# Fourteen modulation units inside three norms, paired units at the first norm, and the step sizes' columns beside the rotated keys

## What is computed

```python
for i in range(DEPTH):                                  # 2 layers
    mod = s_lat @ w_mod[i] + b_mod[i]                   # 1024 -> 6 * 1024
    mod_c = s_ctx @ w_mod[i] + b_mod[i]
    x, xc = _layer(x, xc, mod, mod_c, rope, i < DEPTH - 1, p)

def _layer(x, xc, mod, mod_c, rope, need_ctx, p):
    sh1, sc1, g1, sh2, sc2, g2 = jnp.split(mod[:, None, :], N_MOD, axis=-1)
    h = _modulate(_rms_norm(x, p['g_pre_mix']), sh1, sc1)        # h * (1 + scale) + shift
    hc = _modulate(_rms_norm(xc, p['g_pre_mix']), csh1, csc1)
    ua, us, um = _split_in(h @ p['w_in'])   # ua: queries, keys/values; um ends with the step sizes dt
    ...                                     # latent attention, short convolution, state-space scan
    y = jnp.concatenate([y_att, y_sc, y_ssd], axis=-1) @ p['w_out']
    x = x + g1 * _rms_norm(y, p['g_post_mix'])
    h = _modulate(_rms_norm(x, p['g_pre_ffn']), sh2, sc2)
    f = jnp.square(jax.nn.relu(h @ p['w_ff1'])) @ p['w_ff2']
    x = x + g2 * _rms_norm(f, p['g_post_ffn'])
```

## Time and profile before

| what | us |
|---|---|
| median of 3 runs | 1782.94 |
| lowest and highest of them | 1777.03 and 1785.53 |
| the profiled execution | 1776.61 |
| its span in the trace | 1774.8 |
| its mean granted clock of PE, share of full speed | 0.927 |

### The profile page before, as it was taken

One profiled execution on the slowest core, in us unless ns is written; L12 is line 12 of the kernel. 1 busy time (PEld: TensorE's weight loads), 2 busy tenths in 40 slices (PEclk: granted clock), 3 DMA queues, 4 the chain that ended last, 5 costly groups with the idle time before them and its releaser, 6 DMA issues.

```text
span 1774.8 us, 25783 instructions
## 1 busy us (share of the span) xinstructions
PE 1586.2 (89%) x10259; PEld 1326.2 (75%) x10259; DVE 992.8 (56%) x1598; ACT 917.6 (52%) x1516; POOL 63.7 (4%) x82
## 2 busy tenths in 40 slices
PE   6799988878999999959989789998999999797697
PEld 3578555646888888837955679997989899786587
DVE  0454557555344444454746676667765766576655
ACT  4553555346232323454555555456776766376646
POOL 3000014000000000000004000000000000000000
PEclk8799997788999999969998789998999999989798
DMA  8423364412323223303355436663644434242232
GB/s 276 146 71 95 119 204 153 142 48 71 119 95 95 95 95 96 108 18 96 119 167 190 143 98 195 198 200 129 218 136 143 143 126 134 97 144 95 72 119 72
DMA packets 221560, 225.40 MB, mean 127 GB/s; under 512 B 6154, under 2 KB 219984, under 8 KB 221392
## 3 DMA queue, kind: packets, MB, share of 16 engines
q1 hardware_dynamic: 220736, 223.63, 39.1%
q0 software_dynamic: 704, 0.12, 0.0%
HBM read 222.68 MB, written 1.05 MB: 126 GB/s over the span
## 4 chain that ended last, share of the span: by engine, by line
PE 75%; ACT 11%; DVE 10%; issue 2%; DMA 1%; SPq 0%; DVEq 0%; ACTq 0%; POOL 0%; POOLq 0%
PE bank L851 20%; PE bank L852 20%; PE bank L853 20%; ACT whi L1330 2%; PE bank L1136 2%; PE bank L876 2%; DVE wlo L1869 2%; PE bank L865 1%; ACT SH L1474 1%; PE bank L1114 1%; PE bank L1192 1%; ACT AP L1731 1%; PE bank L1029 1%; PE bank L1021 1%; DVE AP L2378 1%
## 5 line engine op out<-in xcount | busy, mean ns | idle before, releaser
L1869 DVE TENSOR_TENSOR wlo<-raw,whi 128x1024 fp32r<-128x1024 f32 (+3 forms) x322 | 389.0, 1208 | 349.4 <-ACT whi L1330 345.1
L1330 ACT ACTIVATE whi<-raw 128x1024 fp32r<-128x1024 f32 (+3 forms) x322 | 337.2, 1047 | 325.6 <-PE bank L853 305.8
L851 PE MATMUL bank<-HH,whi 128*128 128x512 f32 (+3 forms) x656 | 254.1, 387 | 29.0 <-DVE HL L1891 27.3
L852 PE MATMUL bank<-HL,whi 128*128 128x512 f32 (+3 forms) x656 | 250.9, 382 | 0.0
L853 PE MATMUL bank<-HH,wlo 128*128 128x512 f32 (+3 forms) x656 | 250.5, 382 | 0.0
L851 PE MATMUL bank<-HA,whi 128*128 128x256 f32 x576 | 167.0, 290 | 18.8 <-DVE wlo L1869 8.7
L851 PEld LDWEIGHTS bank<-HH,whi 128*128 128x128 f32 (+2 forms) x656 | 123.6, 188 | 61.6 <-issue 22.3
L852 PE MATMUL bank<-LA,whi 128*128 128x256 f32 x576 | 164.0, 285 | 0.0
L853 PE MATMUL bank<-HA,wlo 128*128 128x256 f32 x576 | 163.9, 284 | 0.0
L853 PEld LDWEIGHTS bank<-HH,wlo 128*128 128x128 f32 (+2 forms) x656 | 123.7, 189 | 26.9 <-issue 1.5
L852 PEld LDWEIGHTS bank<-HL,whi 128*128 128x128 f32 (+2 forms) x656 | 123.9, 189 | 26.1 <-issue 1.8
(11 more groups left out here) (365 smaller groups left out, 3217.1 us busy)
## 6 DMA issues: line engine op xcount, KB each, us to landing
raw<-in_w_ff_dram SPq DMA_DIRECT2D x64, 1024.0 KB, 5.2
raw<-in_w_mod_dram SPq DMA_DIRECT2D x48, 1024.0 KB, 5.2
raw<-in_a_w_in_dram SPq DMA_DIRECT2D x40, 1024.0 KB, 5.0
raw<-in_w_in_dram SPq DMA_DIRECT2D x16, 1024.0 KB, 5.2
raw<-in_b_w_in_dram SPq DMA_DIRECT2D x9, 1024.0 KB, 5.3
raw<-in_w_out_dram SPq DMA_DIRECT2D x8, 1024.0 KB, 5.1
raw<-in_ple_w_gate_dram SPq DMA_DIRECT2D x8, 1024.0 KB, 5.1
raw<-in_a_w_out_dram SPq DMA_DIRECT2D x4, 1024.0 KB, 5.0
```

Of the source, the lines that this page charges most:

```text
L851: nc.tensor.matmul(o, wh, xh, start=start, stop=False, skip_group_check=shared)
L852: nc.tensor.matmul(o, wh, xl, start=False, stop=False, skip_group_check=shared)
L1330: f(whi[h % HALF_SLOTS][:, 0:n], raw[u.id % RAW_SLOTS][:, (h % 2) * n:(h % 2) * n + n], ACT.Copy)\
L1869: v.tensor_tensor(wlo[h % HALF_SLOTS][:, 0:n], raw[u.id % RAW_SLOTS][:, (h % 2) * n:(h % 2) * n + n], whi[h % HALF_SLOTS][:, 0:n].bitcast( ...
```

## The change

It has five parts.

1. The 16 columns of dt are loaded beside the 160 of "kv" by a second transfer into the same slot (runs of 16 values, 64 bytes); the block of 32 becomes one of 48, and "bc" loses its third block. dtT is copied from rows 32 to 47 of the kv block's bank.
2. Fourteen modulation units leave the attention, the scan and w_ff2, and stand inside three norms: 5 in the norm between w_out and w_ff1 of layer 0, 5 in the one between the layers, 4 in the one before w_ff1 of layer 1. They use banks 3 to 6. Two stand before `post`'s sum, one after it, the rest between `norm_sum` and `norm`; ACT and DVE do their rows' work after `post` (two), before `norm_sum` (one) and after `norm` (the rest). The first two weight units after the norm are created and split before `post`. So 19 units stay in layer 0's attention and scan (7 and 12), none in w_ff2, none in layer 1's attention, 7 in layer 1's scan.
3. At the first norm the units come in pairs (shift and scale of the same features), between parts of the sum of squares; kv is split before the last three arrive, the norm is cut in two halves of four feature blocks, and the first half of kv (by feature block) and of q stand between them, with unit 7.
4. `post` no longer adds the last two squares into ACC: PE sums ACC and the two squares. The last two gates are multiplied after the root.
5. The raw slots shrink from 272 to 256 columns a unit.

```diff
 FILL = {
-    "mla": ((1, (1, 8)), (1, (1, 24))),
-    "g": ((1, (1, 8)), (1, (1, 24))),
-    "head": ((1, (1, 8)), (1, (1, 24))),
-    "out": ((1, (1, 8)), (1, (1, 24))),
+    "mla": ((1, (1, 8)), (0, (1, 24))),
+    "g": ((1, (1, 8)), (1, (1, 20))),
+    "head": ((1, (1, 8)), (1, (1, 20))),
+    "out": ((1, (1, 8)), (1, (1, 20))),
 }
+MLA_FILLED = 7
...
+    def kv_unit(l):
+        fm(A["w_in"][l], 0, COL_KV, 160, [(0, P), (P, 48)], "win", (l, "kv"), ("h", l, "mix"), [ALL] * 2, None, [(COL_DT, 16)])
...
-        fm(w, 0, COL_XBC + 512, 272, two + [(256, 16)], "win", (l, "bc"), x, [ALL] * 3)
+        fm(w, 0, COL_XBC + 512, 256, two, "win", (l, "bc"), x, [ALL] * 2)
...
+    one_mod(0)
+    one_mod(4)
+    steps.append(("sum_part", 0, 3))
+    one_mod(1)
+    steps.append(("sum_part", 3, 6))
+    one_mod(5)
+    steps.append(("sum_part", 6, KC))
+    u_kv = without_step(kv_unit, 0)
+    steps.append(("split_to", u_kv))
+    one_mod(2)
+    one_mod(6)
+    one_mod(3)
+    steps.append(("mod_flush",))
+    for j in range(3):
+        steps.append(("fuse_pair", j))
+    steps.append(("norm", 0, "mix", (0, 4)))
+    steps.append(("first_half", u_kv))
+    one_mod(7)
+    u_q = without_step(q_unit, 0)
+    steps.append(("split_to", u_q))
+    steps.append(("first_block", u_q, 0))
+    steps.append(("mod_flush",))
+    steps.append(("fuse_pair", 3))
+    steps.append(("first_block", u_q, 1))
+    steps.append(("norm", 0, "mix", (4, KC)))
...
+        first = [without_step(ff1_unit, 0, i) for i in (0, 1)]
+        made = gap_mods(5 if l == 0 else 4)
+        for u in made[:2]:
+            steps.append(("mod_mm", u))
+        steps.append(("split_to", first[1]))
         steps.append(("post", l, "mix"))
+        for u in made[:2]:
+            steps.append(("mod_rest", u))
+        for u in made[2:3]:
+            steps.append(("unit", u))
         steps.append(("mod_fuse", l, "ffn"))
         steps.append(("norm_sum", l, "ffn"))
-        steps.append(("norm", l, "ffn"))
+        for u in made[3:]:
+            steps.append(("mod_mm", u))
+        steps.append(("norm", l, "ffn", (0, KC)))
+        for u in made[3:]:
+            steps.append(("mod_rest", u))
...
         def post(l, which):
             t = t_of(l)
-            total(s_norm_sum, ("p", l, which), ACC[:, t[0]:t[1]], t[1] - t[0], s_acc, ("p", l, which, KC - 1), (s_inv, ("p", l, which)))
+            b = acquire(7, (s_inv, ("p", l, which)))
+            pe.wait_ge(s_acc, s_acc.at(("p", l, which, KC - 3)))
+            nc.tensor.matmul(b[:, 0:t[1] - t[0]], ones, ACC[:, t[0]:t[1]], start=True, stop=False)
+            for m in (KC - 2, KC - 1):
+                pe.wait_ge(s_sq, s_sq.at(("p", l, which, m)))
+                ins = nc.tensor.matmul(b[:, 0:t[1] - t[0]], ones, SQ[m % 2][:, t[0]:t[1]], start=False, stop=m == KC - 1)
```

More of the change, by code:

```diff
@@ L48 @@
 RAW_SLOTS, HALF_SLOTS = 3, 4
[L49 removed]
+UNIT_COLS = 256
 AHEAD = 4
@@ L457, in build, with fm @@
     units, steps = [], []
-    def fm(w, rows, col, n, blocks, kind, key, x, t, between=None):
-        src = w[rows:rows + D, col:col + n].rearrange("(k p) n -> p k n", p=P)
-        u = Unit(kind, [(0, 8 * n, src)], n, key, len(units), blocks, x, t)
+    def fm(w, rows, col, n, blocks, kind, key, x, t, between=None, more=()):
+        cols = [(col, n), *more]
+        n = sum(m for _, m in cols)
+        loads, at_ = [], 0
+        for c, m in cols:
+            loads.append((0, 8 * n, at_, m, w[rows:rows + D, c:c + m].rearrange("(k p) n -> p k n", p=P)))
+            at_ += m
+        u = Unit(kind, loads, n, key, len(units), blocks, x, t)
         units.append(u)
@@ L496, in build, with q_unit, without_step @@
     two = [(0, P), (P, P)]
+    def kv_unit(l):
+        fm(A["w_in"][l], 0, COL_KV, 160, [(0, P), (P, 48)], "win", (l, "kv"), ("h", l, "mix"), [ALL] * 2, None, [(COL_DT, 16)])
+    def q_unit(l):
+        fm(A["w_in"][l], 0, 0, 256, two, "win", (l, "q"), ("h", l, "mix"), [ALL if l == 0 else X] * 2)
+    def without_step(make, *args):
+        n = len(steps)
+        make(*args)
+        del steps[n:]
+        return units[-1]
     def w_in_units(l):
@@ L581, in build @@
         steps.append(("mod_flush",))
-        steps.append(("post", l, "ffn"))
+        if l == 0:
+            gap_units = [without_step(kv_unit, 1), without_step(q_unit, 1)]
+            made = gap_mods(5)
+            for u in made[:2]:
+                steps.append(("mod_mm", u))
+            steps.append(("split_to", gap_units[1]))
+        else:
+            gap_units, made = [], []
+        steps.append(("post", l, "ffn"))
+        for u in made[:2]:
+            steps.append(("mod_rest", u))
+        for u in made[2:3]:
+            steps.append(("unit", u))
+        for u in first + gap_units if l == 0 else first:
+            u.apart = True
     seq2 = [(0, SEQ)] * 2
@@ L663, in build @@
     mla_last = {l: (l, MLA_HEADS - 1, 1) for l in range(LAYERS)}
-    mod_step = {st[1].key: n for n, st in enumerate(steps) if st[0] == "unit" and st[1].kind == "mod"}
+    mod_step = {st[1].key: n for n, st in enumerate(steps) if st[0] in ("unit", "mod_rest") and st[1].kind == "mod"}
     def half_size(u):
@@ L795, in _ @@
                     sp.wait_ge(s_lo_ready, s_lo_ready.at(2 * before.sid + 1))
-            for off, width, src in u.loads:
+            for off, width, c, m, src in u.loads:
                 dst = raw[u.id % RAW_SLOTS][:, off:off + width].rearrange("p (k n) -> p k n", n=u.n)
-                load(dst, src, raw_in[u.id % RAW_SLOTS])
+                with nc.allow_non_contiguous_dma(reason="sixteen columns of step sizes"):
+                    load(dst[:, :, c:c + m], src, raw_in[u.id % RAW_SLOTS])
             if u.kind == "win" and u.key == (1, "kv"):
@@ L899, in unit @@
                 pe.wait_ge(s_lo_ready, s_lo_ready.at(2 * u.sid + half))
-                for bi, (c0, m) in enumerate(u.blocks):
+                turns = [(bi, kk) for bi in range(len(u.blocks)) for kk in range(4)]
+                if u.by_k:
+                    turns.sort(key=lambda at_: at_[1])
+                for bi, kk in turns:
+                    c0, m = u.blocks[bi]
+                    if only is not None and bi != only:
+                        continue
                     t = u.t[bi]
                     token_major = u.kind == "av" or (u.kind == "bkv" and bi == 1)
-                    if half == 0:
+                    if half == 0 and kk == 0:
                         if u.packed and bi == 0:
@@ L1129, in ssd_out, with norm_sum @@
             ssd_total(l, 1, acquire(4, (s_inv, ("ssd", l, 1))))
-        def norm_sum(l, which):
+        def norm_sum(l, which, k0=0, k1=KC):
             t = ALL if which == "mix" else t_of(l)
-            b = acquire(7, (s_inv, ("n", l, which)))
-            for k in range(KC):
+            b = acquire(7, (s_inv, ("n", l, which))) if k0 == 0 else banks[7]
+            for k in range(k0, k1):
                 pe.wait_ge(s_sq, s_sq.at(("n", l, which, k)))
@@ L1266, in _ @@
                 norm_sum(*args)
+            elif kind == "sum_part":
+                norm_sum(0, "mix", *args)
             elif kind == "rows":
@@ L1410, in unit @@
                         f(ZS[:, 2 * int(part[1]) + bi, t[0]:t[1]], ps, ACT.Silu).then_inc(*key(u.key + (bi,)))
-                    elif part == "bc" and bi == 2:
-                        f(dtT[0:16, :], ps, ACT.Copy).then_inc(*key(u.key + (bi,)))
                     else:
@@ L2542, in _ @@
             if kind == "norm":
-                l, which = args
-                t = ALL if which == "mix" else t_of(l)
-                if which == "mix":
+                l, which, some = args
+                if which == "mix" and some[0] == 0:
                     if l > 0:
```

184 lines of the change are left out of this document (129 added, 55 removed).

## The result

The changed kernel takes **1786.39 us** (median of 20; 1782.77 to 1788.49), the kernel before 1779.95 (20 runs in turn with it): a ratio of 1.0030, 95% interval 1.0017 to 1.0043. It is slower by 0.3%, a small difference but a measured one. I had forecast 1758. In the profiled executions the spans are 1784.9 against 1774.8 us, 10.1 apart.

What follows compares the result with a forecast made beforehand. PE was taken as the bound, three quarters of the chain. Terms -11.1 - 17.7 + 3.6 - 2 + 3.0 - 0.8 = -25.0 gave 1751.6 from the profiled 1776.6, 1758 against the median 1782.94; forecast 1751 to 1764, range 1744 to 1773.

Steps and rivals of the forecast that it cites:

- part 3: Units' cost inside three norms: +3.6 us in sum; those behind norm_sum cost 0, as PE waited 6.75 there.
- rival D: Three norms and the first: mod_rows on ACT behind late loads hold up the norms; slower, about 1785; chance 0.04.
- Parts 2 and 3: Fourteen units leave attention, w_ff2 and layer 1's scan, -17.7 us; their cost inside the norms, +3.6.
- -2 for the clock: Three norms: units in the waits may keep the granted clock up; -2 us, out of 0 to -6.8.
- The third unit: In the three norms: its load lands 5.2 us after issue and squares queue behind it; +0.3, 0 and +3.3 us.
- point (d): Granted clock at the first products after each norm: 0.5 by the forecast, 1.0 by rival B.
- rival B: Norms stay warm: the clock holds at 2.4 GHz there, the first norm too; 1748 us; chance 0.16.
- Part 1: w_in's dt block: four stretches of 2.77 us go, second transfer hidden; -11.1 us (-9 to -11.1).
- Part 5: First norm: first product earlier, -1.9 us, rest up to q's end longer, +4.9; net +3.0 (-1 to +5.5).
- (e): First norm: first product at about 53, q ends at 88, some 4 us wait for HL before kv's second half.
- Part 6: Last post: saves an add and the gates ahead of the root; -0.8 us (0 to -1).
- parts 2, 3 and 4: Units out of dense stretches, -17.7 us; units inside the norms, +3.6; the clock in three norms, -2.

Runs made afterwards that it cites:

- e1: The changed kernel with the second and third units' column products inside the three norms sent to banks 4 and 5, not the rotating banks; 1768.6 us, ratio 0.9939.
- e4: As e1, but no modulation units inside the norms, all fourteen back in the dense stretches; 1770.7 us, ratio 0.9962.
- e3: As e1, but with the first norm of the kernel before; 1765.5 us, ratio 0.9919.
- e9: The kernel before plus the step sizes' columns and the changed post norm, no units in norms, old first norm; 1768.9 us, ratio 0.9928.
- e5: As e3, with the first two units of each of the three norms behind the post norm's sum, on PE only; 1765.2 us, ratio 0.9923.
- e6: As e5, with two units moved from layer 1's norm to the first two steps of layer 1's attention; 1761.9 us, ratio 0.9909.
- e7: As e3, plus 20 unread f32 products, ten ahead of the scores in each of the first two steps of layer 1's attention; 1774.4 us, ratio 0.9978.
- e11: As e8, with the last columns' flush and the gate's fusing moved behind w_out's first unit in both layers; 1757.8 us, ratio 0.9851.
- e8: As e5, with four units per norm, none between post norm and norm's sum, and two in layer 1's attention; 1752.5 us, ratio 0.9852.
- e2: The kernel before with only the step sizes' columns beside the keys and the smaller slots; 1770.9 us, ratio 0.9955.

## Why the prediction was wrong

**The step that failed: part 3, "and PE waited 6.75 there: 0".** I priced the units behind norm_sum by their length on PE against PE's idle time, and asked whether their loads were there. I did not ask where their columns go and when they leave. Each flush takes one of the three banks that the weight products rotate through, and only DVE's copy frees it, which stands behind the norm in DVE's order. The order of the instructions, which I had, shows three flushes ahead of ff1's first product and their copies behind the last HL. The forecast gave this nothing; e1 measures it at 16 us. My rival D had rows on ACT that hold up the norms; it was a queue, a wait and the right sign, but the wrong engine, and the loads were not as late as it needed: the first square came 1.5 us late in layer 0 and 4.5 in layer 1, about as priced with 5.2 us a load. That its 1785 lies next to the measured 1786 is luck: its sum takes the loss of 6.8 us four times, where its text names three norms, and with three it gives 1778.

**Parts 2 and 3, the fourteen units.** I had -17.7 outside, +3.6 inside and -2 for the clock, together -16.1. By the ratios, e1 against e4 gives -4 and e3 against e9 -2. By stages of e3 against e9:
- w_ff2 -1.3 (forecast -1.5): right. Layer 0's attention -5.8 (-5.6) and layer 1's scan -2.2 (-2.4) look right, but by luck. Against e9's 182.6 the same attention is 2.6 to 3.7 us shorter in e5, e6, e7 and e11, and with the new first norm 2.7 (e4 186.4, e1 183.7). The scan with two units less is 1.7 longer than in the kernel before (65.1 against 63.4).
- Layer 1's attention **-4.7, forecast -8.2**. I treated the heads' waits only as time freed or not. Seven units less let PE idle at their head, and the granted clock, 1.00 with a unit in each step, fell to 0.52 over ten us in e3. e6 shows that the first two units there cost 0.2 us together.
- Inside the norms **+12.8, forecast +3.6**: 4.3, 3.1 and 5.5. The third unit was named as the one that decides, and its wait read right (4.60 us on PE; in layer 1 ACT's first square is at 1031.25, 35.7 us behind w_out's first product where it was 31.2, 4.5 late against 4 forecast). Its price was not: e8, without it and with two units back in the attention, has +0.9, +1.1 and -0.3. In layer 0 I took the first square as 1.3 us late and that as made up by XT's last blocks at the end. Nothing was made up: the sixteen records of the sum of squares take 9.6 to 9.7 us on PE with the third unit as without it, and from w_out's first product to the first one behind the norm it is 75.1 us in e3 and 72.0 in e9 and e8. The other 1.1 us at each of the two norms ahead of w_ff1 are a term that I left out. The last two units' flushes stand in the middle of w_ff1, where PE has no wait (timeline of PE, e3):

```profile
425.13 0.95 PE L958 MATMUL bank<-pick,mod_row 128*128 128x2 f32 x8
```

- The clock: at the first product after layer 0's norm it is at the low level, 0.77 us at 400.09 in e1 as at 403.75 before, and with the banks mended the products stay slow for 11.2 us, as before. There point (d) came out as forecast, rival B did not, and the -2 was not there either. Layer 1's norm is different, and (d) fails there: the first product takes 0.36 us, nearer to the 0.28 of the full clock, and the next group starts with 0.58, in the kernel before and in the changed one alike, so nothing was gained (timelines of PE, before and after):

```profile
1032.60 0.36 PE L851 MATMUL bank<-HX,whi 128*128 128x256 f32 x1 [4.13 <-DVE HXL L1891]
...
1042.42 0.36 PE L962 MATMUL bank<-HX,whi 128*128 128x256 f32 x1 [2.59 <-DVE HXL L2037]
1044.04 0.58 PE L962 MATMUL bank<-HX,whi 128*128 128x256 f32 x1 [1.02 <-DVE HXL L2037]
```

The Trainium skill ("TensorE: Matmul & The Clock Gate", Part 1) has the clock fall with idleness. I had weighed that rule only where units go in; e3's trace (0.52 at the head of layer 1's attention) agrees with it where they were taken out, too.

**Part 1, the columns.** -11.1 forecast, -8.0 measured (e2), and -10.0 in the stretches themselves. Layer 1 gave 5.5 us, just the two stretches of 2.77. Products, blocks and the hidden transfer were right; what was missing is that a scan whose clock swings can return some of it.

**Part 5, the first norm.** +3.0 forecast, +3.6 and +3.0 measured, and 3.4 by QC's last copy. First product at 53.26 (52.9 forecast), QC's last copy at 89.5 (88). Both signs of (e) nearly held, though the wait before kv's second half was 1.78 us and not 4:

```profile
53.26 0.77 PE L962 MATMUL bank<-HH,whi 128*128 128x512 f32 x1 [5.18 <-DVE HL L2037]
...
59.70 0.50 PE L962 MATMUL bank<-HH,whi 128*128 128x512 f32 x1 [1.78 <-DVE HL L2037]
```

**Part 6, the last post.** -0.8 forecast. e9 has it over e2, with the earlier split of the two weight units behind a norm; it gives -0.0027 or -5 us, with intervals as wide; by the stages it is -0.3, -2.3, +1.6 and -1.1, together -2.1.

**The sum.** Measured by ratios: -8.0 (columns), +3.6 (first norm, e1 against e3), -4 (units, e1 against e4) and +16 (banks) leave about -2 for the post norm out of the whole of +5.3. With the banks mended (e1) the kernel gains 10.9 us by its ratio where I forecast 25. Of the 14 that are missing, parts 2, 3 and 4 account for 12 (-4 for -16.1) and part 1 for 3, and the post norm gives 1 to 2 back; the wrong sign comes from the banks alone. That is also how the range should have been built: D's mechanism, a queue that PE meets at the end of a norm, deserved more than 0.04, and the range should have reached over it.

What stays open: what lets the clock in a scan swing one way or the other, worth 3 to 5 us in layer 1; and how much of e8's advantage over e5 is the third unit alone, since two units in the attention and one less in the scan came with it. The stages give 5.5 us to it and to the fifth unit, which went with it, in layer 0's two norms.

## What to carry to other kernels

Before work is put into a wait, write down for each piece not only what it takes on the idle engine but every buffer that it holds and the instruction that frees it, with that one's place in its own queue: three copies, 0.55 us together, behind a norm closed three banks for 18 us. Work whose load cannot be there in time does not belong between two sums, and in two norms four units that were ready were worth more than five of which one was late. Filler in a stretch of short waits may be almost free (0.2 us for two units here), so take it out last.

## What the runs showed of the hardware

- Layer 1's scan took 63.4 us before, 66.8 in e2 and 67.4 in e9 with the same nine units in it. In three stretches of 11 us the granted clock was 0.54, 1.00 and 0.74 before, and 0.73, 0.66 and 0.53 in e2.
- Twenty products of f32 operands with 512 columns took 17.2 us at the full clock (granted clock 1.00 from 884 to 904 in e7), 0.86 each, where those of rounded operands take 0.23 at that clock.
- Three waits in a row on PE of 4.60, 0.38 and 18.16 us were followed by products at 0.77 us; after e1's 4.57, 0.37 and 3.68 us it was 0.77 as well. In this norm it made no difference to the first product's pace how long the last wait was.
- Behind the same wait of 2.72 us on PE, four scores of layer 1's attention took 1.95 us in the kernel before and 1.96 in e8, but 2.82 in e3 and 2.80 in e6.
- The bank rule of the Trainium skill ("Perfetto Trace Analysis", Matmul Optimizations) that all eight PSUM banks should be used agrees with e1: three rotating banks, with banks 4 and 5 standing free beside them, cost 16 us.
